# Attention taken two pieces at a time, with one transpose bank and no drain between head pairs

## The chip, the cores and the metric

The kernel runs on one core of a Trainium2 chip. The metric is device time in microseconds of one execution. The kernel before takes 3029.09 us (median of three runs, 3027.73 to 3030.66). Five engines with their own instruction queues work side by side: TensorE (PE; PEld is its weight load), VectorE (DVE), ScalarE (ACT), GpSimd (POOL) and SyncE (SP), which only issues DMAs here. They wait for each other by semaphores.

## The reference

Three blocks run on one sequence of 1024 tokens with 1024 channels: a first hybrid block, a second one with an RWKV branch and an attention branch, and a gated mixing block. The change touches only the attention branch of the second block: 16 heads of 64 channels, and for each head three patterns, with dilations 1, 4 and 16:

```python
DILATED_PATTERNS = ((128, 1), (512, 4), (2048, 16))
# for each pattern: queries in blocks of 128, keys of this block and the one before
s = jnp.einsum('bdhnqe,bdhnke->bdhnqk', qb, kc) * (E ** -0.5)
s = jnp.where(valid, s, -jnp.inf)
m = jnp.max(s, axis=-1, keepdims=True)
pexp = jnp.exp(s - m)
l = jnp.sum(pexp, axis=-1, keepdims=True)
o = jnp.einsum('bdhnqk,bdhnke->bdhnqe', pexp, vc) / l
lse = (m + jnp.log(l))[..., 0]
# the three patterns are weighted with each other
wts = jax.nn.softmax(jnp.stack(lses, axis=0), axis=0)
o = jnp.sum(wts[..., None] * jnp.stack(outs, axis=0), axis=0)
return o.reshape(B, S, ATT_W) * jax.nn.silu(gate)
```

q, k and the gate are projections of the normalised input by `w_in`.

## The kernel before, in words

**Work.** The attention stage takes the heads in eight pairs (p = 0 to 7), two heads on the upper and lower 64 partitions. For a pair there are ten *pieces* (`PIECES`, n = 0 to 9): four of pattern 0 (`pi` 0) and four of pattern 1, with two query blocks each, and two of pattern 2, with four query blocks each. One half of a piece, one head of it, is called a *side* below. A piece goes through these steps:

1. scores (PE, L2333): q times k for both heads into two PSUM banks of the ring `RS`;
2. minimum (DVE, L2498): mask added, written to `Pm`, minimum of each row kept (the sign of the scores is turned round);
3. exponential (ACT, L2430): in place in `Pm`, with the sum of each row;
4. turn (PE, L2346): 128x128 transposes of `Pm` into banks of the ring `RT`, three or four on a side;
5. copy (DVE, L2510): from the turn bank to `PT` in SBUF;
6. values (PE, L2359): `PT` times the values, into a bank of the ring `RO`, where two pieces of patterns 0 and 1 make a group of four blocks; the group is then copied out by ACT (L2442).

**Units.** Beside this PE computes three *units* in each pair: q and k of the next pair and the gate of this one (`att_units_pe`). A unit is 48 matmuls of 512 columns (L259, L260, L261), in eight steps of six. ACT and DVE split its weights first (`w_hi`, L319, and `w_lo`, L327), ACT copies its result out (L363).

**Tail.** When a pair is done, SP writes its row statistics to DRAM and reads them back in another layout (`stats_move`), DVE and ACT make the weights of the three patterns from them (L2528 to L2540), PE turns these (L2373), SP moves them through DRAM to a broadcast tile `MB` (`weights_move`), and DVE scales the outputs (L2547), adds them (L2552), and multiplies by the gate (L2560). All of it stands in the instruction streams of the pair behind.

**POOL** reorders q and k of the next pair for patterns 1 and 2 (`perm_pool`, L2284): two copies for each pattern, once the present pair's last scores of that pattern are done. `perm` has one buffer for each pattern.

**Order.** The order of each engine's instructions is fixed when the program is built. Every part is a generator that yields `STEP`; `weave` takes one turn of each of its generators after another, so that what stands between two `STEP`s, in main, tail and units, in this order, forms one *round*. The same rounds hold on all engines. `paced(gen, n, m)` spreads n steps of a generator over m rounds. Before, a pair's main has 13 times 3 = 39 rounds: a round with scores of piece i, one with the turn of piece i-2, one with the values of piece i-3. The units fill the first 24 of them (8 steps for each of 3). The last 15 hold no unit. Pair 7 has two units, paced over every other round. Behind pair 7 the stream goes on with four units of the next stage (`prep_behind_pe`), 32 rounds, beside the tail of pair 7, and ends in a barrier.

Of the kernel before, what the change touches and what calls it, by code (L numbers as in the profile page):

```python
# [2315 lines left out]

def att_pe_main(K, B, p):
    nc, pe = K.nc, K.pe
    for i in range(NS + 3):
        if i < NS:  # L2320
            s = PIECES[i]
            qk = [B.qkg[:, p % 2, x, :] if s.pi == 0 else B.perm[:, s.pi - 1, x, :] for x in range(2)]
            banks = [B.RS.take(("a_s", p, i, h), ("a_max", p, i, h)) for h in range(2)]
            if s.pi == 0:
                pe.wait_ge(*(yield "uev", ATT_W0 + att_unit(p, 1), 1))
            else:
                pe.wait_ge(*(yield "perm", p, s.pi))
            for _, old in banks:
                if old:
                    pe.wait_ge(*(yield old))  # L2330
            for c, two, lo, hi in s.cells:
                for rr, (bank, _) in zip(RH, banks):
                    a = nc.tensor.matmul(bank[:, lo:hi], qk[0][rr, half(c, 128)],  # L2333
                                         qk[1][rr, 128 * (c - 1) if two else 128 * c:128 * c + 128], start=True,
                                         stop=True)
            a.then_inc(*pe.done("a_s", p, i))
# [1 line left out]
        if 0 <= i - 2 < NS:
            n, s = i - 2, PIECES[i - 2]
            banks = [B.RT.take(("a_t", p, n, h), ("a_pt", p, n, h)) for h in range(2)]  # L2340
            pe.wait_ge(*(yield "a_exp", p, n))
            for h, (bank, old) in enumerate(banks):
                if old:
                    pe.wait_ge(*(yield old))
                for x, b in enumerate(s.blocks):
                    a = nc.tensor.transpose(bank[:, half(x, 128)], B.Pm[:, (NS * p + n) % 3, h, b[0]:b[0] + 128], K.ident)  # L2346
                a.then_inc(*pe.done("a_t", p, n, h))
        yield STEP
        if 0 <= i - 3 < NS:
            n, s = i - 3, PIECES[i - 3]  # L2350
            if s.first:
                ob, old = B.RO.take(("a_o", p, s.pi, s.gg), ("a_osc", p, s.pi, s.gg))
                if old:
                    pe.wait_ge(*(yield old))
            pe.wait_ge(*(yield "a_pt", p, n, 1))
            pe.wait_ge(*(yield "vc", p, s.pi))
            for x, (lo, c, kc, new, end) in enumerate(s.blocks):
                for h, rr in enumerate(RH):
# [1533 lines left out]
```

## Time and profile before

| | us |
|---|---|
| median of 3 runs | 3029.09 |
| profiled execution | 3025.99 |
| its span, first to last instruction | 3024.7 |
| PE busy (share of the span) | 2816.0 (93%) |
| DVE busy | 1654.0 (55%) |
| ACT busy | 1261.6 (42%) |
| POOL busy | 361.0 (12%) |
| granted PE clock, mean | 0.976 |

The attention stage runs from 1092.3 us to 1663.4 us of the span, with the four units behind it. A row of a timeline gives start in us, duration in us, engine, line, operation, the tiles written and read, and xN where N instructions of one kind were merged; idle time of the engine before it and what ended it stand in brackets. Matmuls overlap in the array, so the distance between two starts tells what an instruction costs, and not its duration. A matmul of f32 operands appears as two records: the program's x4 is the timeline's x8. Transposes are one record each.

### The profile page before, as it was taken

What the parts mean: (1) busy time and instruction counts of PE and PEld (TensorE: products, weight loads), DVE (VectorE), ACT (ScalarE), POOL (GpSimd) and SP (SyncE); (2) the same over time, 40 slices, a digit from 0 to 9 for tenths busy, and PEclk for the clock granted to TensorE, in tenths of its full rate; (3) what the DMA queues carried; (4) which work ended last, traced back from release to release, by engine and by line L of the source; (5) the groups of instructions that cost most, each with busy time, mean ns of one, the idle gap of its engine ahead of it and who ended that gap; (6) DMA issues with size and microseconds to landing.
All of it is one profiled execution on the core that took longest, in us unless ns stands there. A gap on an engine that the chain in (4) does not pass through costs nothing. (4 is left out here: it accounts for less than half of the span.)

```text
span 3024.7 us, 52664 instructions
## 1 busy us (share of the span) xinstructions
PE 2816.0 (93%) x21272; PEld 2197.5 (73%) x21272; DVE 1654.0 (55%) x3101; ACT 1261.6 (42%) x2314; POOL 361.0 (12%) x525
## 2 busy tenths in 40 slices
PE   8999999999998999999999999996878899999998
PEld 6767777776666777677777777775777777778776
DVE  3555665753466435655555465574566664652565
ACT  4343534332134445555563443442444334532234
POOL 0000000000000011111110047764440000000000
PEclk9999999999999999999999999998998999999999
DMA  3011111224234532233332335347433464421114
GB/s 117 28 42 36 36 56 35 64 64 171 79 105 139 170 112 72 72 80 86 79 93 66 123 124 169 127 141 284 144 114 138 142 217 132 153 80 45 35 63 153
DMA packets 188369, 316.58 MB, mean 105 GB/s; under 512 B 78288, under 2 KB 119520, under 8 KB 186464
## 3 DMA queue, kind: packets, MB, share of 16 engines
q1 hardware_dynamic: 188128, 313.23, 32.7%
q8 instruction: 168, 2.75, 0.4%
q14 instruction: 73, 0.60, 0.1%
HBM read 239.19 MB, written 73.99 MB: 104 GB/s over the span
## 5 line engine op out<-in xcount | busy, mean ns | idle before, releaser
L259 PE MATMUL ps<-xs,wparts 128*128 128x512 f32 (+1 forms) x1664 | 699.3, 420 | 11.8 <-DVE xs L1528 9.3
L261 PE MATMUL ps<-xs,wparts 128*128 128x512 f32 (+1 forms) x1664 | 654.8, 394 | 0.0
L260 PE MATMUL ps<-xs,wparts 128*128 128x512 f32 (+1 forms) x1664 | 654.1, 393 | 0.0
L327 DVE TENSOR_TENSOR wparts<-wring,wparts 128x1024 fp32r<-128x1024 f32 x248 | 305.7, 1233 | 318.7 <-ACT wparts L319 295.2
L259 PEld LDWEIGHTS ps<-xs,wparts 128*128 128x128 f32 (+1 forms) x1664 | 313.5, 188 | 134.7 <-issue 72.1
L319 ACT ACTIVATE wparts<-wring 128x1024 fp32r<-128x1024 f32 x248 | 263.3, 1062 | 283.2 <-PE ps L261 220.0
L261 PEld LDWEIGHTS ps<-xs,wparts 128*128 128x128 f32 (+1 forms) x1664 | 312.7, 188 | 71.8
L260 PEld LDWEIGHTS ps<-xs,wparts 128*128 128x128 f32 (+1 forms) x1664 | 314.1, 189 | 58.6 <-issue 3.9
L2284 POOL COPY perm<-qkg 128x1024 f32<-128x1024 f32 x32 | 63.1, 2009 | 1488.7 <-ACT qkg L363 1092.0
L2430 ACT ACTIVATE Pm<-Pm,ml 128x128 f32<-128x128 f32 (+1 forms) x384 | 168.5, 442 | 140.9 <-DVE ml L2498 140.9
L2498 DVE CUSTOM_DVE_ANT_0 Pm<-ps,mask 128x128 f32<-128x128 f32 (+1 forms) x384 | 110.9, 348 | 187.9 <-PE ps L2333 187.9
L1787 POOL TENSOR_TENSOR solve<-solve,step 64x30 f32<-64x30 f32 (+14 forms) x240 | 150.6, 628 | 18.8
L1783 POOL TENSOR_TENSOR step<-solve 64x30 f32<-64x30 f32 (+14 forms) x240 | 145.5, 606 | 18.8
L259 PE MATMUL ps<-wparts,mixA 128*128 128x512 f32 x320 | 131.3, 410 | 11.5 <-DVE wparts L327 8.6
L261 PE MATMUL ps<-wparts,mixA 128*128 128x512 f32 x320 | 128.7, 402 | 0.0
L260 PE MATMUL ps<-wparts,mixA 128*128 128x512 f32 x320 | 128.7, 402 | 0.0
L259 PE MATMUL ps<-wparts,xs 128*128 128x512 f32 x256 | 105.2, 411 | 16.7 <-DVE wparts L327 12.9
L2510 DVE COPY PT<-ps 128x384 f32<-128x384 f32 (+1 forms) x160 | 92.2, 618 | 30.3 <-PE ps L2346 30.3
L1423 DVE COPY_PREDICATED h<-lm,ps 128x512 f32<-128x512 uint8 x112 | 82.8, 739 | 38.3 <-PE ps L834 29.4
L259 PE MATMUL ps<-mixA,wparts 128*128 128x512 f32 x256 | 102.3, 400 | 1.0 <-DVE wparts L327 1.0
L260 PE MATMUL ps<-wparts,xs 128*128 128x512 f32 x256 | 102.4, 400 | 0.0
L261 PE MATMUL ps<-wparts,xs 128*128 128x512 f32 x256 | 102.3, 400 | 0.0
(411 smaller groups left out, 4856.3 us busy)
## 6 DMA issues: line engine op xcount, KB each, us to landing
wring<-in_wo SPq DMA_DIRECT2D x96, 512.0 KB, 3.5
ops<-rw SPq DMA_DIRECT2D x32, 640.0 KB, 6.0
wring<-in_w SPq DMA_DIRECT2D x39, 512.0 KB, 3.5
wring<-in_w2u SPq DMA_DIRECT2D x33, 512.0 KB, 4.4
wring<-in_wg SPq DMA_DIRECT2D x24, 512.0 KB, 3.5
wring<-in_w2v SPq DMA_DIRECT2D x24, 512.0 KB, 4.1
wring<-in_w2a SPq DMA_DIRECT2D x24, 512.0 KB, 6.6
MB<-wst SPq DMA_DIRECT2D x48, 256.0 KB, 5.0
```

The costliest lines, as they stand in the source:

```text
L259: nc.tensor.matmul(out, a, c, start=start, stop=False)
L260: nc.tensor.matmul(out, b, c, start=False, stop=False)
L261: return nc.tensor.matmul(out, a, d, start=False, stop=stop)
L319: K.nc.scalar.activation(W.part(i, 0), W.raw(i), ACT.Copy).then_inc(*K.act.done("w_hi", W.first + i))
L327: K.nc.vector.tensor_tensor(W.part(i, 1), W.raw(i), W.part(i, 0).bitcast(F32), ALU.subtract).then_inc(*K.dve.done("w_lo", W.first + i))
L1423: a = nc.vector.copy_predicated(dst, B.lmask[:, lev, :].unsqueeze(1).to_broadcast([128, 4, 128]), src)
L1783: nc.gpsimd.tensor_tensor(d, G[:, 0:s, s:s + 1].to_broadcast([64, s, n]), G[:, s:s + 1, s + 1:32].to_broadcast([64, s, n]), ALU.mult).then ...
L1787: nc.gpsimd.tensor_tensor(G[:, 0:s, s + 1:32], G[:, 0:s, s + 1:32], d, ALU.add).then_inc(*pool.done("step_add", p, s, also=[("solved", p)] ...
L2284: nc.gpsimd.tensor_copy(B.perm[:, pi - 1, x, :].rearrange("p (r j) -> p r j", r=r), B.qkg[:, p % 2, x, :].rearrange("p (j r) -> p r j", r= ...
L2430: a = nc.scalar.activation(P, P, ACT.Exp, scale=-1.0, bias=ml[:, s.pi, c, h, 0:1], accum_out=ml[:, s.pi, c, h, 1:2])
L2498: a = nc.vector.tensor_tensor_reduce(B.Pm[:, (NS * p + i) % 3, h, lo:hi], K.bank["a_s", p, i, h][:, lo:hi], m, 1.0, 3e38, ALU.add, ALU.min ...
L2510: nc.vector.tensor_copy(B.PT[:, (NS * p + n) % 2, h, 0:w], K.bank["a_t", p, n, h][:, 0:w]).then_inc(*dve.done("a_pt", p, n, h))
```

## The change

Pieces are taken in *duos*: five duos for a pair (g = 5p to 5p+4), of two pieces or four sides (j = 0 to 3). The rounds of a duo are seven. In the first, PE does the values of both pieces of the duo two back (g-2) and then the scores of both pieces of this one. In the second to fifth it turns one side each of the duo before (g-1). The sixth and seventh hold nothing of main. DVE does the minimum of side j in rounds 1 to 4, and behind it in rounds 2 to 5 the copy of the side turned there. ACT does the exponential of one side in each of rounds 2 to 5. The duos of a pair follow those of the pair before without a gap; two more groups of seven rounds stand behind pair 7 (`main(K, B, 8)`). The units of a pair are paced at two steps in three rounds, 24 steps over 36 rounds, so that rounds 3, 6, 9 and so on hold no unit. Scores have four PSUM banks, turns one, values one; the second half of pattern 2's values goes to the turn bank. `Pm` has six sides, as before. The values of pattern 2 are loaded later in SP's stream. The rounds of the tail stay, except that the turn of the weights (PE) and its copy (ACT) stand one round later.

```diff
@@ -1813,7 +1813,7 @@
 def prep_behind_pe(K, B, p):
...
-    B.RU = at.RU.join(at.RS)
+    B.RU = at.RU.join(at.RS.part([0, 1]))
...
@@ -1869,7 +1869,7 @@
...
-    B.RM = at.RT.join(at.RO)
+    B.RM = at.RT.join(at.RO, at.RS.part([2, 3]))
...
@@ -2117,7 +2117,7 @@
...
-    B.PT, B.Pm, B.Vc = sb("PT", [128, 2, 2, 512]), sb("Pm", [128, 3, 2, 512]), sb("Vc", [128, 24, 128])
+    B.PT, B.Pm, B.Vc = sb("PT", [128, 2, 2, 512]), sb("Pm", [128, 6, 512]), sb("Vc", [128, 24, 128])
...
@@ -2160,10 +2160,28 @@
...
+ND2 = NS // 2
+
+
+def duo(g):
+
+    return divmod(g, ND2) if 0 <= g < 8 * ND2 else None
+
+
+def side(g, j):
+
+    (p, d), (x, h) = duo(g), divmod(j, 2)
+    return p, 2 * d + x, h
+
+
+def shelf(B, g, j):
+
+    return B.Pm[:, (4 * g + j) % 6, :]
+
+
+def duos(p):
+
+    return range(ND2 * p, ND2 * p + (ND2 if p < 8 else 2))
...
@@ -2191,6 +2209,7 @@
...
             if p and i == 3 * p + 4:
+                yield from values_load(K, A, B, p, 2)
                 yield from weights_move(K, A, B, p - 1)
...
         yield from stats_move(K, A, B, p)
-        for pi in (1, 2):
-            if p < 7:
-                yield from values_load(K, A, B, p + 1, pi)
+        if p < 7:
+            yield from values_load(K, A, B, p + 1, 1)
...
@@ -2235,7 +2253,7 @@
...
-    sp.wait_ge(*(yield "a_exp", p, NS - 1))
+    sp.wait_ge(*(yield "a_exp", p, NS - 1, 1))
...
+def values_pe(K, B, p, n):
+    nc, pe, s = K.nc, K.pe, PIECES[n]
+    if s.first:
+        ring = B.RT if (s.pi, s.gg) == (2, 1) else B.RO
+        _, old = ring.take(("a_o", p, s.pi, s.gg), ("a_osc", p, s.pi, s.gg))
+        if old:
+            pe.wait_ge(*(yield old))
+    ob = K.bank["a_o", p, s.pi, s.gg]
...
+def turn_pe(K, B, g, j):
+    nc, pe, (p, n, h) = K.nc, K.pe, side(g, j)
+    bank, old = B.RT.take(("a_t", p, n, h), ("a_pt", p, n, h))
+    pe.wait_ge(*(yield "a_exp", p, n, h))
+    if old:
+        pe.wait_ge(*(yield old))
+    for x, b in enumerate(PIECES[n].blocks):
+        a = nc.tensor.transpose(bank[:, half(x, 128)], shelf(B, g, j)[:, b[0]:b[0] + 128], K.ident)
+    a.then_inc(*pe.done("a_t", p, n, h))
+
+
 def att_pe_main(K, B, p):
...
+    for g in duos(p):
+        for x in range(2):
+            if duo(g - 2):
+                yield from values_pe(K, B, *side(g - 2, 2 * x)[:2])
+        for x in range(2):
+            if duo(g):
+                yield from scores_pe(K, B, *side(g, 2 * x)[:2])
+        yield STEP
+        for j in range(4):
+            if duo(g - 1):
+                yield from turn_pe(K, B, g - 1, j)
+            yield STEP
+        for _ in range(2):
+            yield STEP
...
-    for _ in range(TURN + 4):
+    for _ in range(TURN + 5):
...
                          *([tail(K, B, p - 1)] if p else []),
-                         units(K, B, p + 1) if p < 7 else paced(fill(K, B), 1, 2))
-    yield from weave(tail(K, B, 7), behind(K, B.prep, 0))
+                         paced(units(K, B, p + 1), 2, 3) if p < 7 else paced(fill(K, B), 1, 2))
+    yield from weave(main(K, B, 8), tail(K, B, 7), behind(K, B.prep, 0))
...
-    B.RS, B.RT, B.RO = rows.part([0, 1]), rows.part([2, 3]), rows.part([4, 5])
+    B.RS, B.RT, B.RO = rows.part([0, 1, 2, 3]), rows.part([4]), rows.part([5])
...
+def exp_act(K, B, g, j):
+    nc, act, (p, n, h) = K.nc, K.act, side(g, j)
+    s, ml, P = PIECES[n], B.ml2[:, p % 2], shelf(B, g, j)
+    if p >= 2:
...
+    for g in duos(p):
+        for x in range(2):
+            if duo(g - 2):
+                q, n, _ = side(g - 2, 2 * x)
+                if PIECES[n].last:
+                    yield from out_act(K, B, q, PIECES[n])
+        yield STEP
+        for j in range(4):
+            if duo(g):
+                yield from exp_act(K, B, g, j)
+            yield STEP
+        for _ in range(2):
+            yield STEP
...
-    for _ in range(4):
+    for _ in range(5):
...
+def turn_dve(K, B, g, j):
+    nc, dve, (p, n, h) = K.nc, K.dve, side(g, j)
+    w = 128 * len(PIECES[n].blocks)
+    if duo(g - 1):
+        dve.wait_ge(*(yield ("a_av", *side(g - 1, j)[:2])))
+    dve.wait_ge(*(yield "a_t", p, n, h))
+    nc.vector.tensor_copy(B.PT[:, n % 2, h, 0:w], K.bank["a_t", p, n, h][:, 0:w]).then_inc(*dve.done("a_pt", p, n, h))
+
+
 def att_dve_main(K, B, p):
...
+    for g in duos(p):
+        for j in range(5):
+            if j < 4 and duo(g):
+                yield from max_dve(K, B, g, j)
+            if j and duo(g - 1):
+                yield from turn_dve(K, B, g - 1, j - 1)
+            yield STEP
+        for _ in range(2):
+            yield STEP
 
```

What this does to the order, at two places. The first is PE's stream at pattern 2's duo, the fifth of a pair. In the kernel before, piece 8's scores (L2333), turns (L2346) and values (L2359) stand there, behind the last six matmuls of the units:

```order
L2333 MATMUL ps<-perm 128x128 x8
L2346 MATMUL ps<-cc,Pm 128x128 x6
L2359 MATMUL ps<-PT,Vc 64x128 x6
L2333 MATMUL ps<-perm 128x128 x8
L2346 MATMUL ps<-cc,Pm 128x128 x6
L2359 MATMUL ps<-PT,Vc 64x128 x6
L2346 MATMUL ps<-cc,Pm 128x128 x8
```

The changed kernel at the same work (scores L2348, turns L2377, values L2365):

```order
L2365 MATMUL ps<-PT,Vc 64x128 x12
L2348 MATMUL ps<-perm 128x128 x16
L259 MATMUL ps<-xs,wparts 128x512
L260 MATMUL ps<-xs,wparts 128x512
L261 MATMUL ps<-xs,wparts 128x512
L259 MATMUL ps<-xs,wparts 128x512
L260 MATMUL ps<-xs,wparts 128x512
L261 MATMUL ps<-xs,wparts 128x512
L2377 MATMUL ps<-cc,Pm 128x128 x6
```

The values and scores of two pieces stand together, six unit matmuls follow, and then two sides' turns (three transposes each) one right behind the other; the second of them needs the bank that the first one filled.

The second place is DVE's stream at the same duo. Before, the tail's addition (L2552) stands behind copies and in front of the next copies:

```order
L2498 ISA ml 128x1
L2510 COPY PT<-ps 128x384 x2
L2552 TENSOR_TENSOR O<-O 128x1024
L2510 COPY PT<-ps 128x512 x2
L2560 TENSOR_TENSOR O<-O,qkg 128x1024
L2510 COPY PT<-ps 128x512 x2
```

In the changed kernel (minimum L2536, copy L2547, the tail's addition L2598, the weight split L327 as before), from the end of side 0's minimum to the first copy of the duo (side 1's minimum is four such pairs of rows, one for each query block, of which one stands):

```order
L2536 ISA ml 128x1
L2598 TENSOR_TENSOR O<-O 128x1024
L327 TENSOR_TENSOR wparts<-wring,wparts 128x1024
L2536 ISA Pm,ml<-ps,mask 128x128
L2536 ISA ml 128x1
...
L2547 COPY PT<-ps 128x384
```

The addition and the split of a unit's weights now stand in front of side 1's minimum and of the first copy out of the one turn bank.

## Rows read from the trace of the kernel before

**Rows 1.** Windows: start:end, length, busy PE, PEld, DVE, ACT, POOL, clock, DMA.
```profile
1092.30:1157.70 65.40, 63.15 (x452) 47.54 (x452) 29.00 (x119) 36.86 (x113) 15.73 (x8) 1.00 0.10 26
1157.70:1558.20 400.50, 379.77 (x2706) 284.52 (x2706) 231.82 (x786) 222.95 (x690) 47.36 (x24) 1.00 0.32 82
1291.20:1343.70 52.50, 52.50 (x324) 38.83 (x323) 27.00 (x88) 25.85 (x78) 4.04 (x2) 1.00 0.38 93
1343.70:1357.90 14.20, 10.74 (x129) 8.56 (x128) 11.65 (x43) 11.30 (x37) 3.87 (x2) 1.00 0.11 39
1558.20:1618.80 60.60, 54.99 (x406) 40.96 (x404) 37.57 (x134) 38.96 (x115) 0.00 (x0) 0.94 0.32 74
1618.80:1663.40 44.60, 44.34 (x197) 36.33 (x196) 18.20 (x22) 12.45 (x16) 0.00 (x0) 1.00 0.31 85
```

**Rows 2.** Timeline of PE in pair 3, rounds that hold unit matmuls.
```profile
1336.53 0.39 PE L261 MATMUL ps<-xs,wparts 128*128 128x512 f32 x1
1336.85 0.93 PE L2333 MATMUL ps<-perm 64*128 64x128 f32 x8
1337.70 0.50 PE L259 MATMUL ps<-xs,wparts 128*128 128x512 f32 x1
...
1339.20 0.82 PE L2346 MATMUL ps<-cc,Pm 128*128 128x128 f32 x6
1339.77 0.47 PE L259 MATMUL ps<-xs,wparts 128*128 128x512 f32 x1
...
1341.01 0.40 PE L261 MATMUL ps<-xs,wparts 128*128 128x512 f32 x1
1341.34 0.88 PE L2359 MATMUL ps<-PT,Vc 128*64 128x128 f32 x12
1342.14 0.50 PE L259 MATMUL ps<-xs,wparts 128*128 128x512 f32 x1
```

**Rows 3.** Timeline of PE in pair 3, the rounds without units.
```profile
1353.79 1.17 PE L2346 MATMUL ps<-cc,Pm 128*128 128x128 f32 x8 [0.71 <-DVE PT L2510]
...
1356.91 1.09 PE L2359 MATMUL ps<-PT,Vc 128*64 128x128 f32 x16 [0.94 <-DVE PT L2510]
1357.94 0.93 PE L2333 MATMUL ps<-qkg 64*128 64x128 f32 x8
```

**Rows 4.** Timeline of DVE in pair 3.
```profile
1334.30 1.23 DVE L327 TENSOR_TENSOR wparts<-wring,wparts 128x1024 fp32r<-128x1024 f32 x1
...
1337.82 0.29 DVE L2498 CUSTOM_DVE_ANT_0 Pm<-ps,mask 128x128 f32<-128x128 f32 x1 [1.03 <-PE ps L2333]
...
1338.04 0.42 DVE L2498 CUSTOM_DVE_ANT_0 Pm<-ps,mask 128x256 f32<-128x256 f32 x1
...
1338.38 0.29 DVE L2498 CUSTOM_DVE_ANT_0 Pm<-ps,mask 128x128 f32<-128x128 f32 x1
...
1339.80 1.02 DVE L2510 COPY PT<-ps 128x384 f32<-128x384 f32 x2 [0.78 <-PE ps L2346]
1340.85 2.19 DVE L2552 TENSOR_TENSOR O<-O 128x1024 f32<-128x1024 f32 x1
...
1352.96 1.28 DVE L2510 COPY PT<-ps 128x512 f32<-128x512 f32 x2
```

**Rows 5.** Timeline of DVE in pair 3, small operations of the tail.
```profile
1306.84 0.25 DVE L2534 TENSOR_TENSOR sums<-w,own 128x48 f32<-128x48 f32 x1 [0.31 <-ACT w L2453]
...
1307.65 0.24 DVE L2540 TENSOR_TENSOR w<-w,top 128x48 f32<-128x48 f32 x1
```

**Rows 6.** Timeline of POOL in pair 3.
```profile
1337.92 4.04 POOL L2284 COPY perm<-qkg 128x1024 f32<-128x1024 f32 x2 [52.75 <-PE ps L2333]
```

**Rows 7.** Windows in pair 7, around a wait of PE.
```profile
1590.00:1593.00 3.00, 0.21 (x1) 0.00 (x0) 1.45 (x10) 0.52 (x4) 0.00 (x0) 0.99 0.02 4
1593.00:1596.00 3.00, 2.67 (x13) 2.01 (x14) 2.83 (x5) 1.95 (x7) 0.00 (x0) 0.50 0.00 0
```

**Rows 8.** Timeline in pair 7, the same wait.
```profile
1591.52 0.18 DVE L1970 TENSOR_SCALAR early<-early 128x25 f32<-128x25 f32 x1 [8.00 <-DMA early<-in_c]
...
1593.15 1.65 PE L2333 MATMUL ps<-perm 64*128 64x128 f32 x8 [2.94 <-DVE ml L2498]
```

**Rows 9.** Timeline of SP, the statistics of pair 3.
```profile
1355.97 3.57 SPq L2247 DMA_DIRECT2D st<-ml  x5
1364.22 0.38 SPq L2251 DMA_DIRECT2D own<-st  x1
```

More of the change, by code:

```diff
@@ L2314, in att_fill_pe @@
     yield from prep_first_pe(K, B.prep, B.RU)
-def att_pe_main(K, B, p):
[L2318 to L2336, printed above, removed]
-        yield STEP
[L2338 to L2358, printed above, removed]
-                    a = nc.tensor.matmul(ob[rr, half(c % 4, 128)], B.Vc[:, 8 * s.pi + kc, rr],
-                                         B.PT[:, (NS * p + n) % 2, h, half(x, 128)], start=new, stop=end,
-                                         skip_group_check=True)
-            a.then_inc(*pe.done("a_av", p, n))
-        yield STEP
@@ new lines, in scores_pe @@
+def scores_pe(K, B, p, i):
+    nc, pe, s = K.nc, K.pe, PIECES[i]
+    qk = [B.qkg[:, p % 2, x, :] if s.pi == 0 else B.perm[:, s.pi - 1, x, :] for x in range(2)]
+    banks = [B.RS.take(("a_s", p, i, h), ("a_max", p, i, h)) for h in range(2)]
+    if s.pi == 0:
+        pe.wait_ge(*(yield "uev", ATT_W0 + att_unit(p, 1), 1))
+    else:
+        pe.wait_ge(*(yield "perm", p, s.pi))
+    for _, old in banks:
+        if old:
+            pe.wait_ge(*(yield old))
+    for c, two, lo, hi in s.cells:
+        for rr, (bank, _) in zip(RH, banks):
+            a = nc.tensor.matmul(bank[:, lo:hi], qk[0][rr, half(c, 128)],
+                                 qk[1][rr, 128 * (c - 1) if two else 128 * c:128 * c + 128], start=True, stop=True)
+    a.then_inc(*pe.done("a_s", p, i))
@@ new lines, in values_pe @@
+def values_pe(K, B, p, n):
[6 more added lines that the diff above has]
+    ob = K.bank["a_o", p, s.pi, s.gg]
+    pe.wait_ge(*(yield "a_pt", p, n, 1))
+    pe.wait_ge(*(yield "vc", p, s.pi))
+    for x, (lo, c, kc, new, end) in enumerate(s.blocks):
+        for h, rr in enumerate(RH):
+            a = nc.tensor.matmul(ob[rr, half(c % 4, 128)], B.Vc[:, 8 * s.pi + kc, rr], B.PT[:, n % 2, h, half(x, 128)],
+                                 start=new, stop=end, skip_group_check=True)
+    a.then_inc(*pe.done("a_av", p, n))
@@ new lines, in exp_act @@
+def exp_act(K, B, g, j):
+    nc, act, (p, n, h) = K.nc, K.act, side(g, j)
+    s, ml, P = PIECES[n], B.ml2[:, p % 2], shelf(B, g, j)
+    if p >= 2:
+        act.wait_ge(*(yield "w_mul", p - 2))
+    act.wait_ge(*(yield "a_max", p, n, h))
+    for c, two, lo, hi in s.cells:
+        a = nc.scalar.activation(P[:, lo:hi], P[:, lo:hi], ACT.Exp, scale=-1.0, bias=ml[:, s.pi, c, h, 0:1],
+                                 accum_out=ml[:, s.pi, c, h, 1:2])
+    a.then_inc(*act.done("a_exp", p, n, h))
@@ new lines, in max_dve @@
+def max_dve(K, B, g, j):
+    nc, dve, (p, n, h) = K.nc, K.dve, side(g, j)
+    s, ml, P = PIECES[n], B.ml2[:, p % 2], shelf(B, g, j)
+    dve.wait_ge(*(yield "a_s", p, n))
+    if 4 * g + j >= 6:
+        dve.wait_ge(*(yield ("a_t", *side(*divmod(4 * g + j - 6, 4)))))
+    if p >= 2:
+        dve.wait_ge(*(yield "w_mul", p - 2))
+    for c, two, lo, hi in s.cells:
+        m = B.mask[:, 256:384] if s.pi == 2 else B.mask[:, 0:256] if two else B.mask[:, 128:256]
+        a = nc.vector.tensor_tensor_reduce(P[:, lo:hi], K.bank["a_s", p, n, h][:, lo:hi], m, 1.0, 3e38, ALU.add, ALU.min,
+                                           ml[:, s.pi, c, h, 0:1])
+    a.then_inc(*dve.done("a_max", p, n, h))
@@ new lines, in turn_dve @@
+def turn_dve(K, B, g, j):
+    nc, dve, (p, n, h) = K.nc, K.dve, side(g, j)
+    w = 128 * len(PIECES[n].blocks)
[3 more added lines that the diff above has]
+    nc.vector.tensor_copy(B.PT[:, n % 2, h, 0:w], K.bank["a_t", p, n, h][:, 0:w]).then_inc(*dve.done("a_pt", p, n, h))
+def att_dve_main(K, B, p):
+    for g in duos(p):
[7 more added lines that the diff above has]
+            yield STEP
```

68 lines of the change are left out of this document (11 added, 57 removed).

## The prediction

> **What bounds the kernel now.** I read the page's shares first: PE is busy in 93% of the span. The windows say where it isn't. The attention stage is seven pairs alike, a pair with half the units, and the four units behind [rows 1]. Pairs 1 to 6 take 400.5 us, 66.75 each: the 24 rounds with unit matmuls take 52.5 us with PE busy all the time, the 15 rounds without take 14.2 us with PE busy for 10.7. DVE is busy for 38.7 us of such a pair (27.0 + 11.65) and ACT for 37.2. So PE's stream sets the pace, and the question is what it loses between its instructions.
>
> For that I took PE's timeline. Unit matmuls follow each other by 0.23 us (the split of 3 x 16 x 3 = 144 in a pair). A piece's scores with two query blocks of 128 and two of 256 columns, both heads side by side in the array, push the next unit matmul from 1336.76 to 1337.70: 0.94 us [rows 2]. Values of three blocks push it from 1341.24 to 1342.14: 0.90 us; six transposes take 0.57 us [rows 2], 0.095 each. Four blocks of values with scores behind them take 1.03 us, four blocks being 16 records [rows 3]. With 0.215 us for 128 columns of both heads these are 0.645 + 0.29, 0.645 + 0.26 and 0.86 + 0.17. So a group of f32 matmuls between unit matmuls costs 0.28 us besides its columns, a change from values to scores 0.17, and a group of transposes nothing. In the rounds without units PE waits for DVE's copies: 0.71 and 0.94 us in two rows [rows 3].
>
> **What the change takes away.** A pair's work on PE is 144 x 0.2275 = 32.8 us of units, 35 blocks of scores and 35 of values x 0.215 = 15.05, 70 transposes x 0.095 = 6.65, and 0.1 for the tail's transpose: 54.6. Five groups of values and scores take the place of twenty of one kind; each costs 0.28 + 0.17 = 0.45, together 2.3. Base of a pair after: **56.9 us**, against 66.75. Up to 9.8 us in a pair is there to be won, if nothing new waits.
>
> **What it adds: one turn bank.** Each turn now waits for the copy of the one before. The chain, from rows: a turn of six transposes in two banks starts at 1339.20, and the copy of its first three starts at 1339.80 [rows 2, 4], 0.60 us; four transposes make it 0.70. A copy of 384 columns takes 0.51 (half of 1.02), of 512 columns 0.64; from the start of the first copy of 512 at 1352.96 to the next turn's start at 1353.79 are 0.83 us [rows 3, 4], so 0.19 for the way back. From turn to turn at least 1.3 us (three) or 1.5 us (four), where the turn itself takes PE 0.29 or 0.38. Six unit matmuls between two turns (1.37 us) cover that. But every third round has none, and five times in a pair two turns stand bare behind each other (sides 1 to 2 of the first duo, 0 to 1 of the second, 2 to 3 of the third, 1 to 2 of the fourth, 0 to 1 of the fifth), and the tail's transpose stands bare behind the last turn of the second duo. Each costs 1.05 us: **6.3 us** a pair.
>
> **What stands in front of the copies on DVE.** DVE does side j+1's minimum and then side j's copy. A minimum costs 0.22 us for 128 columns and 0.34 for 256 [rows 4]: 0.56 or 0.68 for a side, 0.85 in pattern 2. With nothing else it is done when the turn is. Whatever else DVE has between two copies, less some 0.3 us of slack, is PE's wait where the turns are bare:
> - second duo: the tail's four small operations, 1.05 us from the first's start to the last's end [rows 5], then a minimum and a copy before the third turn: **0.6**.
> - third duo: the split of a weight (1.23 us [rows 4]) between the copy of side 1 and the minimum in front of copy 2, before a bare turn: **0.7** over the bare turn's own 1.05.
> - fourth duo: the addition, 1.23 us without contention, in front of minimum 2 and copy 1: **0.55** more.
> - fifth duo: the addition and the split, both in front of minimum 1 (0.85) and copy 0. Counted from the duo's start, scores of side 0 start at 0.1 + 1.29 (six blocks of values) + 0.17 = 1.55, the minimum starts 0.97 to 1.18 behind (1336.85 to 1337.82 in [rows 2, 4]), say at 2.7, and ends at 3.6. Then 1.23 + 1.23 + 0.85 + 0.51 + 0.19 brings turn 1 to 7.6. PE was ready at 5.1 (scores to 3.2, six unit matmuls, turn 0). A wait of 2.5, of which 1.05 is the bare turn's: **1.5** more.
>
> POOL comes on top. Its two copies for pattern 2 start when the last scores of that pattern are done, at about 3.6, the moment at which DVE comes to the addition. In the kernel before, an addition that began at 1340.85 took 2.19 us, not 1.23; POOL's copies had begun at 1337.92 and ran 4.04 us, to 1341.96; the addition ended at 1343.04, 1.08 us behind them [rows 4, 6]. Such an addition waits out POOL's copy. The split has the same form (two inputs in SBUF, 128x1024, the same 1.23 us), but in the trace it never meets a copy. The bounds are 0 (DVE always gets in first) and 4.0 us (both copies of 2.0 first); I take one copy, **2.0**, since the meeting is a tie. Fourth duo: a POOL copy holds up L2593 behind copy 2, where nothing waits for it: 0. The Trainium skill ("SBUF — State Buffer", "SBUF: two separate sides") says that a VectorE operation with two SBUF inputs and a GpSimd operation that reads SBUF exclude each other for the whole instruction. The addition's 2.19 us agrees; of the split no run here shows it. By that rule the 2.0 us stand, by the split's own rows (always 1.23) they might fall to 1 or less.
>
> **The clock.** Turn 1 of the fifth duo then leaves PE idle for some 4 us. Before, PE waited 2.94 us once in pair 7, behind a DVE wait for a load, and the granted clock stood at 0.50 in the 3 us after it, the lower level of 1.2 GHz [rows 7, 8]. I take 3.4 us at half clock in each pair, **1.7 us** lost; the bounds are 0 and 3.4.
>
> Sum of a pair: 56.9 + 6.3 + 0.6 + 0.7 + 0.55 + 1.5 + 2.0 + 1.7 = 70.25, rounded up to **70.4** for the small waits that I can't place. Against 66.75 that is +3.65, times six pairs: **+22**.
>
> **The other edits.** Pair 0 has no tail, and no values or turns of a pair before: 65.4 us now [rows 1], and 56.9 less 3.0 (14 blocks of values), 1.5 (16 transposes) and 0.1, with four bare turns (4.2) and 0.7: 57. **-8.** Pair 7 has 16 unit rounds among 35: 16 x 1.37 + 15.05 + 2.3 + 6.7 = 46; nine bare places (9.5), DVE's addition and split together in front of a bare turn (2), and the constants that DVE waits 8.0 us for [rows 8], which now meet one bank and a bare turn (5 and 2 of clock): 65 against 60.6 [rows 1]. **+5.** The last values and turns, 14 blocks and 16 transposes with two groups, move in among the four units: 3.0 + 1.5 + 0.6 and the tail of pair 7 behind them: **+6** on 44.6. The statistics take 8.6 us from the first issue to the read back and some 2 more [rows 9]; they start at round 33 and are asked for at round 8 of the next pair, some 15 us later: nothing, with 4 us of slack. The later load of pattern 2's values and the one round later turn of the weights: nothing. The shelf of six sides in `Pm` asks for a turn that DVE has already waited for: nothing.
>
> Total: +22 - 8 + 5 + 6 = **+25 us**. The profiled execution took 3025.99 us (span 3024.7), the median is 3029.09; to the median this is **3054 us**.
>
> **The rivals.**
> - *The waits hide, faster.* DVE's extra work falls into slack, as the copies of 0.5 us might come early enough, and only the bare turns cost: 56.9 + 6.3 = 63.2 a pair, -3.5 x 6 - 8 + 3 + 6 = -20: 3009 us. For it speaks that DVE has a third of its time free; against it, that its order is fixed and the tail's operations stand right in front of copies. It decides from the point where the wait in the fifth duo stays under 1.5 us. 17%.
> - *POOL and clock do nothing.* DVE wins the tie and the clock holds: 66.7 a pair, +3 in all: 3032 us. Against it speaks [rows 4, 6] and [rows 7]. 18%.
> - *Worse.* Both POOL copies go first, PE idles for 6 us and the clock stays low for longer (+2.0 and +1.7), pair 73.5: about +45: 3074 us. 15%.
> - My forecast, 3054 us, from 3040 to 3068: 50%.
>
> A measurement of this kernel can tell 0.2% (6 us) from no change. Faster by more than that: the first rival and an edge of the second, 0.20. Within it: 0.12. Slower: 0.68. The range takes in part of the first rival and the last: 3014 to 3078 us.
>
> **What would show it.** A pair's period in the trace: near 70 against 66.75. PE's waits for DVE's copies in front of the turns: five or six longer than 1 us in a pair, the longest, above 3.5 us, in the fifth duo. DVE's addition or split there longer than 2 us, beside POOL's copy. Clock rows of 0.50 once in a pair. The unit matmuls 0.23 us apart as before. Wrong I am if the turns wait less than 8 us in a pair in all, or if the period falls under 65.

## The result, and the profile after

The changed kernel takes 3078.08 us (median of four runs, 3076.47 to 3083.07) against 3029.88 us for the kernel before (3027.73 to 3033.97): ratio 1.0162, 95% interval 1.0147 to 1.0178. It is 48 us slower. I had forecast 3054 us in a range of 3014 to 3078: the direction was right, the size too small by half, and the time lies just outside the range.

The profiled execution has a span of 3076.6 us, 51.9 more than before. From the page of the kernel after (busy time, share, instructions; below it the group of the turns: busy, mean ns of one, idle time in front and what ended it):

```profile
PE 2802.0 (91%) x21272; PEld 2209.0 (72%) x21272; DVE 1681.1 (55%) x3101; ACT 1278.3 (42%) x2328; POOL 372.2 (12%) x525
L2377 PE MATMUL ps<-cc,Pm 128*128 128x128 f32 x560 | 93.7, 286 | 85.4 <-DVE PT L2547 83.6
```

The 560 transposes (160 turns of three or four) have 85 us of idle time in front of them, nearly all ended by DVE's copy. The windows of the kernel after, to be held against [rows 1] (start:end, length, busy PE, PEld, DVE, ACT, POOL, granted clock, DMA), are pair 0, pairs 1 to 6, pair 7, and what comes behind up to the barrier:

```profile
1093.60:1156.70 63.10, 57.41 (x402) 45.73 (x403) 28.77 (x115) 36.13 (x112) 17.77 (x8) 0.97 0.10 26
1156.70:1599.64 442.94, 374.47 (x2708) 297.59 (x2707) 257.16 (x786) 238.91 (x702) 53.13 (x24) 0.96 0.29 74
1599.60:1665.80 66.20, 49.65 (x367) 38.89 (x366) 32.70 (x115) 34.36 (x93) 0.00 (x0) 0.90 0.25 59
1665.80:1720.40 54.60, 52.16 (x280) 42.40 (x280) 26.66 (x46) 19.98 (x42) 0.00 (x0) 1.00 0.30 80
```

Pairs 1 to 6 take 73.8 us each (442.94/6) where 66.8 were needed: 42.4 of the 51.9 us. PE is busy for 62.4 us of such a pair, even 0.9 less than before (63.3), and idle for 11.4, against 3.5. The clock is 0.96 instead of 1.00. Pair 0 gained 2.3 us, and the stage began 1.3 us later, in work that wasn't changed. Pair 7 and what stands behind it lost 16.0. Their end is the first unit matmul behind the barrier, before and after:

```profile
1663.02 0.47 PE L259 MATMUL ps<-xs,wparts 128*128 128x512 f32 x1 [0.26 <-issue]
1720.43 0.47 PE L259 MATMUL ps<-xs,wparts 128*128 128x512 f32 x1 [0.27 <-issue]
```

From 1558.2 to 1663.0 are 104.8 us, from 1599.6 to 1720.4 are 120.8. What follows took 5.5 us less than before (1356.2 against 1361.7). Over all profiled executions here it took 1353 to 1368 us, so this is no gain to be put down to the change, and the time of a pair tells kernels apart better than the time of the whole.

What ended PE's waits in pairs 1 to 6 (kernel after; us in total, times, longest):

```profile
PE ps L2377 <- DVE PT L2547: 62.4, 35, 5.5
PE ps L2405 <- DVE PT L2547: 5.3, 6, 0.9
PE ps L2377 <- ACT Pm L2457: 0.8, 1, 0.8
```

And the seven waits of one pair, the fourth, as PE's timeline has them (start, length, instruction, idle time before it):

```profile
1310.25 0.63 PE L2377 MATMUL ps<-cc,Pm 128*128 128x128 f32 x4 [0.88 <-DVE PT L2547]
1322.00 0.52 PE L2377 MATMUL ps<-cc,Pm 128*128 128x128 f32 x3 [0.81 <-DVE PT L2547]
1324.29 0.63 PE L2377 MATMUL ps<-cc,Pm 128*128 128x128 f32 x4 [0.38 <-DVE PT L2547]
1327.62 0.27 PE L2405 MATMUL ps<-cc,w 128*48 128x128 f32 x1 [0.88 <-DVE PT L2547]
1339.70 0.63 PE L2377 MATMUL ps<-cc,Pm 128*128 128x128 f32 x4 [1.54 <-DVE PT L2547]
1351.49 0.52 PE L2377 MATMUL ps<-cc,Pm 128*128 128x128 f32 x3 [1.37 <-DVE PT L2547]
1367.37 0.88 PE L2377 MATMUL ps<-cc,Pm 128*128 128x128 f32 x3 [5.51 <-DVE PT L2547]
```

Six of the seven stand where no unit matmul lies between a turn and the one before it; the small one at 1324.29 stands behind DVE's small operations of the tail. The longest is in the fifth duo. DVE's timeline in front of that turn, without the repeated minima:

```profile
1359.74 0.29 DVE L2536 CUSTOM_DVE_ANT_0 Pm<-ps,mask 128x128 f32<-128x128 f32 x1
...
1360.07 3.00 DVE L2598 TENSOR_TENSOR O<-O 128x1024 f32<-128x1024 f32 x1
1363.18 2.73 DVE L327 TENSOR_TENSOR wparts<-wring,wparts 128x1024 fp32r<-128x1024 f32 x1
1365.83 0.28 DVE L2536 CUSTOM_DVE_ANT_0 Pm<-ps,mask 128x128 f32<-128x128 f32 x1
...
1366.68 0.55 DVE L2547 COPY PT<-ps 128x384 f32<-128x384 f32 x1
```

POOL's timeline beside it (x2: two copies in a row):

```profile
1360.02 4.80 POOL L2302 COPY perm<-qkg 128x1024 f32<-128x1024 f32 x2 [5.47 <-PE ps L2348]
```

POOL begins 0.05 us before DVE's addition. The addition takes 3.00 us and the split 2.73, where each takes 1.23 with POOL still ([rows 4] for the split). Only then come the minima of side 1 and the copy that frees the bank. The windows around the wait:

```profile
1362.00:1365.00 3.00, 0.00 (x0) 0.00 (x0) 2.90 (x2) 0.00 (x0) 2.83 (x1) 1.00 0.00 0
1365.00:1368.00 3.00, 0.63 (x4) 0.66 (x4) 3.00 (x18) 1.21 (x7) 0.00 (x0) 0.56 0.00 0
1368.00:1371.00 3.00, 3.00 (x10) 2.31 (x9) 1.46 (x11) 2.92 (x12) 0.00 (x0) 0.50 0.00 0
1371.00:1374.00 3.00, 3.00 (x15) 2.50 (x14) 0.96 (x2) 2.96 (x7) 0.00 (x0) 0.80 0.03 8
```

PE is idle, the granted clock falls to 0.50 (1.2 of 2.4 GHz), and it is still there when PE works again.

### The profile page after: what moved, and what is told of

It reads as the page before. It is cut to its first block and busy times, and to the rows that moved or that the text cites. A ratio compares the mean times of both kernels' runs of the same rounds, so it can differ in the third digit from the quotient of the medians.

```text
span 3076.6 us, 52717 instructions
## 1 busy us (share of the span) xinstructions
PE 2802.0 (91%) x21272; PEld 2209.0 (72%) x21272; DVE 1681.1 (55%) x3101; ACT 1278.3 (42%) x2328; POOL 372.2 (12%) x525
## 5 line engine op out<-in xcount | busy, mean ns | idle before, releaser
L327 DVE TENSOR_TENSOR wparts<-wring,wparts 128x1024 fp32r<-128x1024 f32 x248 | 316.6, 1277 | 311.8 <-ACT wparts L319 288.4
L259 PEld LDWEIGHTS ps<-xs,wparts 128*128 128x128 f32 (+1 forms) x1664 | 317.2, 191 | 119.2 <-issue 55.2
L261 PEld LDWEIGHTS ps<-xs,wparts 128*128 128x128 f32 (+1 forms) x1664 | 316.3, 190 | 73.5
L260 PEld LDWEIGHTS ps<-xs,wparts 128*128 128x128 f32 (+1 forms) x1664 | 317.6, 191 | 59.3 <-issue 3.8
L2302 POOL COPY perm<-qkg 128x1024 f32<-128x1024 f32 x32 | 70.9, 2249 | 1515.4 <-ACT qkg L363 1477.4
L2536 DVE CUSTOM_DVE_ANT_0 Pm<-ps,mask 128x128 f32<-128x128 f32 (+1 forms) x384 | 114.3, 346 | 157.4 <-PE ps L2348 157.4
L2377 PE MATMUL ps<-cc,Pm 128*128 128x128 f32 x560 | 93.7, 286 | 85.4 <-DVE PT L2547 83.6
L2377 PEld LDWEIGHTS ps<-cc,Pm 128*128 128x128 f32 x560 | 69.5, 146 | 114.7 <-issue 74.3
L2547 DVE COPY PT<-ps 128x384 f32<-128x384 f32 (+1 forms) x160 | 99.7, 623 | 95.2 <-PE ps L2377 94.3
L259 PE MATMUL ps<-wparts,xs 128*128 128x512 f32 x256 | 105.7, 413 | 17.0 <-DVE wparts L327 13.4
```

Source lines behind the costliest of these rows:

```text
L259: nc.tensor.matmul(out, a, c, start=start, stop=False)
L260: nc.tensor.matmul(out, b, c, start=False, stop=False)
L261: return nc.tensor.matmul(out, a, d, start=False, stop=stop)
L327: K.nc.vector.tensor_tensor(W.part(i, 1), W.raw(i), W.part(i, 0).bitcast(F32), ALU.subtract).then_inc(*K.dve.done("w_lo", W.first + i))
L2377: a = nc.tensor.transpose(bank[:, half(x, 128)], shelf(B, g, j)[:, b[0]:b[0] + 128], K.ident)
L2536: a = nc.vector.tensor_tensor_reduce(P[:, lo:hi], K.bank["a_s", p, n, h][:, lo:hi], m, 1.0, 3e38, ALU.add, ALU.min, ml[:, s.pi, c, h, 0:1])
```

## The experiments

Theory: the loss of a pair is the sum of the waits in front of the turns (one bank behind DVE's fixed order), the stretching of DVE's operations beside POOL's copies, and the clock behind the longest wait; PE's work itself became shorter. Its main rivals were that the waits only replace each other, and that the change's grouping by duos is what costs. Each time below is a median; the table at the end of this section has the parts of a pair for all.

**POOL out of the way.** In the kernel after, POOL's two copies for pattern 2 wait for the split too.

```diff
             pool.wait_ge(*(yield "a_s", p - 1, LAST[pi]))
+        if p and pi == 2:
+            pool.wait_ge(*(yield "w_lo", ATT_W0 + 3 * p + 2))
```

> One added wait on POOL: its copies for pattern 2 start only when DVE has done the weight split of the fifth duo. Theory (DVE's addition and split there wait out POOL's two copies, and the long idle time of PE then halves the clock): the addition and the split return to 1.23 us each, PE's longest wait for a copy falls from 5.5 to about 2.3 us, the clock rows of 0.50 in pairs 1 to 6 go, a pair falls from 73.8 to about 68.5 us, the kernel from 3078 to about 3043 us. Rival (DVE's order alone makes the wait, POOL runs beside it): the wait stays above 4.5 us and the kernel at 3072 or more. Second rival (the exclusion counts, but the clock falls for other reasons): 3056 us, with the 0.50 rows still there.

Measured: 3045.36 us (3042.67 to 3058.47), ratio to the kernel before 1.007 (1.0045 to 1.0095); 69.2 us a pair. DVE's timeline in that kernel, and its turn behind it on PE:

```profile
1346.78 1.23 DVE L2600 TENSOR_TENSOR O<-O 128x1024 f32<-128x1024 f32 x1
1348.11 1.23 DVE L327 TENSOR_TENSOR wparts<-wring,wparts 128x1024 fp32r<-128x1024 f32 x1
```

```profile
1350.79 0.87 PE L2379 MATMUL ps<-cc,Pm 128*128 128x128 f32 x3 [2.23 <-DVE PT L2549]
```

The wait fell from 5.51 to 2.23: by 3.28 us, which is what the two operations lost beside POOL (1.77 + 1.50 = 3.27). So each of them waits for one of the two copies. In the kernel after, the split ends at 1365.91, 1.09 us behind POOL's second copy (1364.82), as the addition of [rows 4, 6] ended 1.08 behind it. It is the only edit, POOL's copies are merely later, and it takes back 33 us of the 48. The Trainium skill ("SBUF — State Buffer", "SBUF: two separate sides") says that such an operation of VectorE and a GpSimd operation that reads SBUF shut each other out; here the split obeys this too, which no trace of before had shown.

This kernel also prices the clock. The forecast that the rows of 0.50 go was only half right: a stretch at 0.50 of some 3.4 us is left in three of the six pairs; those pairs take 69.99, 69.86 and 69.99 us, the others 68.41, 68.43 and 68.77. So such a stretch costs 1.4 us. One of its windows:

```profile
1351.00:1354.00 3.00, 3.00 (x10) 2.35 (x10) 1.88 (x15) 2.92 (x14) 2.32 (x2) 0.51 0.00 0
```

**Units where the turns are.** In the kernel after, `fitted` takes one step of the units in each round of a list: the 24 steps of a pair stand in the first five of each duo's seven rounds (in the third duo the first is left out), instead of in two of every three rounds.

```diff
...
-                         paced(units(K, B, p + 1), 2, 3) if p < 7 else paced(fill(K, B), 1, 2))
+                         fitted(units(K, B, p + 1), FIT) if p < 7 else paced(fill(K, B), 1, 2))
...
+FIT = [7 * d + x for d in range(5) for x in range(5) if (d, x) != (2, 0)]
```

> The 24 unit steps of a pair stand in rounds 1 to 5 of each duo (all but one), so that no turn stands bare behind another; nothing else moves. Theory (one turn bank costs about 1 us wherever two turns have no units between them, six times a pair): the waits of 0.8 to 1.5 us in front of turns go in duos 1 to 4, the fifth duo's falls by the 1.4 us of units; a pair falls by 5 to 7 us, the kernel to about 3040 us. Rival (turns wait for DVE's amount of work, not for the bank's way there and back): the waits stay in sum and move to other turns; the kernel stays within 10 us of 3078.

Measured: 3028.48 us (3025.0 to 3036.95), ratio 1.0001 (0.9987 to 1.0014); 66.6 us a pair. The bare turns' waits are gone (one of 0.2 us is left, in front of values); the fifth duo's remains, 4.12 us, with the clock at 0.50 behind it:

```profile
1342.22 0.87 PE L2398 MATMUL ps<-cc,Pm 128*128 128x128 f32 x3 [4.12 <-DVE PT L2568]
```

**DVE's extra work moved.** In the kernel after, the three splits of a pair stand in rounds 5, 19 and 33, and the tail's scalings and additions in rounds 18 to 27, so that they are apart from each other.

```diff
...
+    for n, i in zip((5, 14, 14), (att_unit(p, 0), att_unit(p, 1), att_unit(p - 1, 2))):
+        for _ in range(n):
+            yield STEP
+        yield from w_lo(K, B.W, i + 1)
...
-        for _ in range(4 if pi == 2 else 2):
+        for _ in range((2, 5, 1)[pi]):
             yield STEP
```

> Only DVE's stream changes: the three weight splits of a pair stand in the sixth round of duos 1, 3 and 5, and the tail's additions behind the last copy of the fourth duo. The bare turns stay. Theory: DVE's extra operations in front of copies cost 0.7 + 0.5 + 1.5 us, and the meeting with POOL and the clock 3.3 + 2 more; the wait in the fifth duo falls to 1.0 us, a pair falls by 8 us to 66, the kernel to about 3025 us, no faster than before. Rival (the bank's way there and back is the larger part): under 4 us a pair, 3055 us or more.

Measured: 3027.44 us (3019.3 to 3031.48), ratio 0.9996 (0.9985 to 1.0008); 65.8 us a pair, no stretch at half clock in pairs 1 to 6, and no wait longer than 0.94 us. Pairs 1 to 6:

```profile
1150.61:1545.24 394.63, 361.98 (x2708) 288.02 (x2707) 233.21 (x786) 238.36 (x703) 47.58 (x24) 1.00 0.33 83
```

**Both.** The two edits above in one kernel.

> The two edits before this one together. Theory (two causes of their own, that add up): a pair falls by 13 to 14 us to about 60, 3 above the base of its matmuls; the kernel to about 2990 us, faster than before. Rival (when these waits go, ACT's exponentials or DVE's 43 us of work in a pair make new ones): a pair stays above 64, the kernel above 3015 us.

Measured: 2981.16 us (2975.47 to 2991.71), ratio 0.9845 (0.9821 to 0.9868); 59.4 us a pair. PE is busy from end to end (first number the length, second PE):

```profile
1150.40:1506.60 356.20, 356.19 (x2708) 287.11 (x2706) 228.91 (x786) 236.79 (x701) 48.02 (x24) 1.00 0.36 90
```

Nothing in the duos or in the one bank needs to wait. The two edits bring 7.2 and 8.0 us alone, 14.4 together: the waits hardly replace each other.

**Spreading alone.** The kernel before, with its 24 unit steps spread over 36 of its 39 rounds, and nothing else.

```diff
-                         units(K, B, p + 1) if p < 7 else paced(fill(K, B), 1, 2))
+                         paced(units(K, B, p + 1), 2, 3) if p < 7 else paced(fill(K, B), 1, 2))
```

> The kernel before, with one part of the change alone: its units at two steps in three rounds over 36 of its 39 rounds; two turn banks, one piece at a time, drain kept. Theory (spreading is good where there are two turn banks, since the 6 us that a pair loses in its rounds without units are covered): a pair falls from 66.75 to about 63.5 us, the kernel from 3029 to about 3007 us. Rival (a group of f32 matmuls between unit matmuls costs more than one next to its like, and cancels it): a pair stays within 1 us of 66.75, the kernel within 8 us of 3029.

Measured: 2994.4 us (2989.63 to 3001.82), ratio 0.9886 (0.9866 to 0.9906); 62.2 us a pair.

```profile
1155.64:1528.56 372.92, 372.92 (x2709) 284.82 (x2707) 235.68 (x786) 223.02 (x691) 47.73 (x24) 1.00 0.35 87
```

Of the change's parts this one gains 35 us by itself, where I expected 22; the others turn it into a loss of 48. The duos shorten PE's work by another 2.8 us a pair (62.2 to 59.4) but only where nothing waits.

**Two banks in one ring.** In the kernel after, turns and values share a ring of two banks, as before the change.

```diff
...
-    B.RS, B.RT, B.RO = rows.part([0, 1, 2, 3]), rows.part([4]), rows.part([5])
+    B.RS, B.RT = rows.part([0, 1, 2, 3]), rows.part([4, 5])
+    B.RO = B.RT
```

> The changed kernel with turns and values taking both banks in turn from one ring of two, in place of one bank each; bare turns, DVE's order and POOL stay. Theory (the bare turns wait for the one bank's way through DVE): the waits of 0.8 to 1.5 us in duos 1 to 4 go, the longest one, in the fifth, moves to the next turn and shrinks by the 1.8 us of work before it; a pair falls from 73.8 by 6 to 8 us, the kernel to about 3033 us. Rival (DVE's queue is what is late, whatever the banks): the waits move on by one turn and keep their sum; within 12 us of 3078.

Measured: 3014.29 us (3009.21 to 3016.99), ratio 0.9948 (0.9933 to 0.9962); 65.3 us a pair, 8.5 less, where 6 to 8 were forecast; the kernel gained 64 us where 45 were forecast, since pair 0 (6.8 us) and pair 7 with what stands behind it (9.2 us) gained too. What is left of the waits in pairs 1 to 6:

```profile
PE ps L2377 <- DVE PT L2548: 23.0, 6, 3.8
PE ps L2405 <- DVE PT L2548: 2.5, 6, 0.4
PE ps L2365 <- DVE PT L2548: 0.3, 1, 0.3
```

The small waits have gone, but for 0.4 us in front of the tail's transpose. The meeting with POOL has not (3.01 and 2.74 us for the addition and the split); the second bank lets PE run one turn ahead and takes 1.7 us off.

**Ring and POOL.** The first and the last of these edits together: does what they bring add up, and is anything else left?

> The kernel after with two of its edits taken back at once: turns and values go through one ring of two banks, as before, and POOL's two copies also wait for the split. Theory (the costs of the one bank and of the meeting with POOL are separate and add): the shared ring alone gave 64.9 us a pair, taking POOL away alone gave 4.6 us a pair (73.8 to 69.24), of which some 1.5 us were half clock that the shared ring already partly removed; so 60 to 61 us a pair and about 2988 us, no stretch at half clock in most pairs. Rival (both shorten the same wait, the turn of the fifth duo, and what one gave the other can't give again): at least 63 us a pair and 3005 us or more.

Measured: 2983.53 us (2980.03 to 2993.8), ratio 0.9846 (0.9822 to 0.9871); 60.4 us a pair. Alone they bring 8.5 and 4.6 us, together 13.4: they add up, as the theory had it. (The 64.9 us a pair that it starts from is 65.3 by the window over all six pairs.) The turn of the fifth duo:

```profile
1323.52 0.52 PE L2379 MATMUL ps<-cc,Pm 128*128 128x128 f32 x3 [0.52 <-DVE PT L2550]
```

From the ring's 3.83 us the wait fell by 3.3, the meeting's price once more. Rounds, units and DVE's order are those of the changed kernel; two small edits take away 95 of its microseconds. Pairs 1 to 6:

```profile
1149.13:1511.45 362.32, 356.49 (x2708) 288.53 (x2706) 225.08 (x786) 237.77 (x701) 52.77 (x24) 1.00 0.36 90
```

**Copy in front of the minimum.** In the kernel after, DVE does side j-1's copy and then side j's minimum.

```diff
-            if j < 4 and duo(g):
-                yield from max_dve(K, B, g, j)
             if j and duo(g - 1):
                 yield from turn_dve(K, B, g - 1, j - 1)
+            if j < 4 and duo(g):
+                yield from max_dve(K, B, g, j)
```

> The changed kernel with each copy in front of the minimum of the same round on DVE. Theory: the minimum counts only where something else on DVE stands before it and the turn is bare: 0.5 to 0.85 us in duos 2 to 5 each; the bare turns' own 0.9 us stay. A pair falls by 2 to 3 us, the kernel to about 3063 us. Rival (the minimum is covered, or the later exponentials cost it again): within 5 us of 3078.

Measured: 3072.27 us (3067.59 to 3073.96), ratio 1.0138 (1.0123 to 1.0154); 73.0 us a pair, only 0.8 less. My theory of the size fails. Only the fifth duo's wait moved, from 5.51 to 4.66, by one side's minima; the small ones stayed within 0.01 us of their value (the same pair's first five in that kernel read 0.88, 0.81, 0.37, 0.88 and 1.53). At the bare turns the minimum is done before the turn is, and the wait is the way from turn to copy to turn alone.

**The last pair.** The kernel with both edits, and pair 7's units set between its turns too, and the load of its constants moved up so that DVE doesn't wait for it.

```diff
+LAST_FIT = [7 * d + x for d in range(5) for x in range(1, 5) if x < 4 or d == 4]
...
-    K.sp.wait_ge(*(yield "a_s", 6, LAST[0]))
-    K.sp.wait_ge(*(yield "perm", 6, 2))
-    K.nc.sync.dma_start(B.cols[:, 0:96], A["c2"]).then_inc(*K.sp.done("c2", by=16))
...
+        if p == 7:
+            sp.wait_ge(*(yield "a_s", 6, LAST[0]))
+            sp.wait_ge(*(yield "perm", 6, 2))
+            nc.sync.dma_start(B.prep.cols[:, 0:96], A["c2"]).then_inc(*sp.done("c2", by=16))
...
-                         (units(K, B, p + 1) if units is att_units_dve else fitted(units(K, B, p + 1), FIT)) if p < 7 else paced(fill(K, B), 1, 2))
+                         (units(K, B, p + 1) if units is att_units_dve else fitted(units(K, B, p + 1), FIT)) if p < 7 else fitted(fill(K, B), LAST_FIT))
```

> The best one so far (e4_both), and in pair 7 the same: its 16 unit steps stand between turns, and the load of the constants that DVE waits for is issued before the others of the pair. Theory: DVE's wait of 7 us for the constants, PE's of 7.1 us behind it and the half clock after it go, pair 7 falls from 66 to about 52 us; the kernel from 2981 to about 2967 us. Rival (the load lands no earlier, since it waits for something else): within 4 us of 2981.

Measured: 2970.21 us (2967.8 to 2971.91), ratio 0.9803 (0.9786 to 0.9819). The wait of 7.09 us in front of a turn of pair 7 is gone; the longest there is 2.28 us.

**The same with the shared ring.**

> The best version so far (units fitted into rounds 1 to 5, splits and tail spread, last pair's units spread and its constants loaded first: 2970.2 us) with the shared ring of two banks as well. Theory (where units stand between the turns the bank for the turn is free in time, so a second bank gains nothing more): 59 to 59.6 us a pair, 2965 to 2973 us. Rival (the small waits for a turn's bank still cost 0.2 us each there, some 6 a pair): 58 us a pair, about 2960 us or less.

Measured: 2966.35 us (2965.06 to 2973.45), ratio 0.9798 (0.9775 to 0.9821); 59.2 us a pair. From the version with one bank this can't be told apart. Both beat the kernel before by 2% and the changed one by 3.5%.

Per pair, mean of pairs 1 to 6, from the window over them in each kernel (idle is length less busy):

| kernel | length | PE idle | PE busy | clock |
|---|---|---|---|---|
| before | 66.8 | 3.5 | 63.3 | 1.00 |
| after | 73.8 | 11.4 | 62.4 | 0.96 |
| after, POOL later | 69.2 | 8.1 | 61.1 | 0.99 |
| after, units between turns | 66.6 | 4.5 | 62.1 | 0.96 |
| after, DVE's work moved | 65.8 | 5.4 | 60.3 | 1.00 |
| both of these | 59.4 | 0.0 | 59.4 | 1.00 |
| before, units spread | 62.2 | 0.0 | 62.2 | 1.00 |
| after, shared ring | 65.3 | 4.3 | 61.0 | 0.97 |
| after, ring and POOL | 60.4 | 1.0 | 59.4 | 1.00 |
| after, copy first | 73.0 | 10.5 | 62.5 | 0.96 |
| both edits, last pair | 59.4 | 0.0 | 59.4 | 1.00 |
| the same, shared ring | 59.2 | 0.0 | 59.2 | 1.00 |

## Why the prediction was right in its mechanism and wrong in its size

A pair takes 73.8 us; I had 70.4. Step by step:

- **Base, 56.9 us: too low by 2.5.** This is the step that failed most. PE's work with hardly a wait, at full clock and in the changed order, is 59.4 us (ring and POOL). I took every unit matmul at 0.2275 us and a turn's group at its columns alone. PE's timeline of the kernel after, at the start of the same pair:

```profile
1305.46 0.50 PE L259 MATMUL ps<-xs,wparts 128*128 128x512 f32 x1
1305.79 0.40 PE L260 MATMUL ps<-xs,wparts 128*128 128x512 f32 x1
1306.03 0.40 PE L261 MATMUL ps<-xs,wparts 128*128 128x512 f32 x1
...
1306.96 0.60 PE L2377 MATMUL ps<-cc,Pm 128*128 128x128 f32 x4
1307.31 0.47 PE L259 MATMUL ps<-xs,wparts 128*128 128x512 f32 x1
1307.62 0.39 PE L260 MATMUL ps<-xs,wparts 128*128 128x512 f32 x1
...
1308.78 0.60 PE L2377 MATMUL ps<-cc,Pm 128*128 128x128 f32 x4
1310.25 0.63 PE L2377 MATMUL ps<-cc,Pm 128*128 128x128 f32 x4 [0.88 <-DVE PT L2547]
```

  The first unit matmul behind any other group takes 0.33 or 0.31 us to the next one instead of 0.23; six take 1.50, not 1.37. There are 19 such restarts in a pair of the ring-and-POOL kernel, 1.7 us in all over 0.2275 each. The same stood in the trace of before: from 1337.70 to the turn at 1339.20 are 1.50 us for six [rows 2]. I had measured the gap in front of the restart and not the one behind it. The rest is in the starts too. In the ring-and-POOL kernel the 144 unit matmuls of a pair take 35.5 us and not 32.8: besides the restarts, the last one in front of another group takes 0.265 us on average (0.7 in all) and the others 0.230 (0.3). Values and scores take 17.1 and not 17.35, turns 6.9 and not 6.75.
- **Waits in front of the turns, 6.3 + 0.6 + 0.7 + 0.55 + 1.5 + 2.0 = 11.65 us: right but for POOL.** PE's idle time is 11.4; what the waits cost is 12.3 (see "The rest"). Idle time by place, forecast and then measured in the fourth pair: first duo 1.05 and 0.88; second 2.7 and 2.07; third 1.75 and 1.54; fourth 1.6 and 1.37; fifth 4.55 and 5.51. A bare turn's idle time reads 0.88 or 0.81 and not 1.05, but its price was as forecast: from one turn's start to the next 1.47 us for four transposes (1308.78 to 1310.25 above) and 1.30 for three (1320.70 to 1322.00), where I had 1.5 and 1.3. That the one bank causes them, two experiments show: a second bank takes them away, and so do units between the turns.
- **POOL's meeting, 2.0 us: too low by 1.3.** I had one copy in the way; both are, one before the addition and one before the split, 3.3 us. Without it the waits cost 9.0 us, where I had 9.65. Its bounds, 0 to 4.0, held.
- **The clock, 1.7 us: too low by some 0.4.** One stretch of 3.4 us costs 1.4 us (POOL later). In the changed kernel four of six pairs have a second such stretch behind the first, and take 74.0 to 74.5 us where the other two take 73.0 and 73.2: 1.1 us more. That makes about 2.1 a pair.
- **The rest.** 59.4 + 11.4 + 2.1 is 72.9. The other 0.9 us belongs to the waits: it is in the turn in front of each. A turn of four takes 0.35 us from its start to a unit matmul's behind it (1306.96 to 1307.31), but is busy for 0.60 where PE waits behind it (1308.78), since no matmul overlaps its end there; for three it is 0.25 and 0.49. The profile's busy ends are modelled, the starts are not. The kernel with DVE's work moved shows the same at clock 1.00: busy for 60.3 against 59.4 in the ring-and-POOL kernel with the same order of PE's work, and all of the difference stands in the turns' rows (7.7 against 6.7 us). So the waits cost 11.4 + 0.9 = 12.3 us.
- **Pair 0, -8 us: it was -2.3.** The base was too low there as well (55.1 us in the ring-and-POOL kernel; I had 52 without waits), and I forgot that the fifth duo's split meets POOL in that pair too, although no tail stands there: the split takes 2.93 us, PE waits 2.67 in front of a turn, and the clock is 0.97.
- **Pair 7 and behind, +5 and +6: too low by 5**, 16.0. The idle time of pair 7 was right: 16.6 us, 16.5 forecast. The wait for the constants was 7.43 us in front of its turn where I had 5, and the small ones were shorter by as much. But six of its unit matmuls (1.5 us) stand behind 1665.8, so the pair took 67.7 us where I had 65, with PE busy for 51.2 where I had 48, 2 of these for the clock. The window's clock of 0.90 over 66.2 us stands for some 13 us at 0.50. How much of the 3 us is clock and how much base stays open. Behind it were 53.1 us where I had 50.6, with waits of 0.8 and 1.4 that I had at nothing.
- **Edits costed at nothing**: the later values' load, the weights' turn and the statistics cost nothing that any wait shows. Nor does the shelf of `Pm`: the one wait for ACT in six pairs, 0.81 us, is a bare turn's, as long as in the other pairs (1.30 us from start to start), where it is put down to DVE.
- **The sum.** Pairs 1 to 6 cost 20 us more than forecast (base 15, POOL 8, clock 2, the other waits 4 less and my rounding up 1 less), pair 0 5.7, pair 7 and behind 5, the later start 1.3; the work behind the stage gave back 5.5. That is 52 for 25.

The signs that I had named came: seven waits, five of them over 0.85 us and the longest 5.51 in the fifth duo, the addition and the split stretched beside POOL, rows of 0.50 in each pair. Only "five or six over 1 us" was wrong, they were three. The rival "worse" (73.5 us a pair, 3074 us) was nearest. Both POOL copies in the way were right in it, but it had 4.0 us for them instead of 3.3 and 3.4 us for the clock instead of 2.1, which made up for a base that it too took as known at 56.9. That it came so near is in part luck; its own terms, 70.25 + 2.0 + 1.7, make 73.95 and not 73.5. The range ended at 3078 because it moved only the terms that I had called unknown.

## What to carry to other kernels

When work is moved so that a stream should run without gaps, price the stream from a stretch of the same length that holds all its kinds (such as 1.50 us from a first unit matmul to the next turn), not from single intervals: here nineteen small restarts (1.7 us) were as large as each of the two terms argued over longest. Count a wait from start to start, since the instruction in front of it also stays busy longer. A single bank between two engines cost nothing here while other work lay between its uses, and the whole way there and back where none did: place the filling work by that, not evenly. Look what stands on DVE in front of the copy that frees it, and whether another engine's reads of SBUF fall on the same moment.
